# A hybrid decoder step on one core: some turned blocks as transposes, two key copies and two low-rank products side by side, a gate chunk split

## The reference, cut to what matters

```python
h  = rms_norm(x) * (1 + scale1) + shift1
q, k, v, p_rw, g_a, g_b = split(h @ w_in)
A  = sliding-window attention(q, k, v)           # window 128, T5 bias, sinks
xm = p_rw + (prev - p_rw) * mu                   # token shift
r, k, v, wl, al, gl = split(xm)
w_log = -softplus(-(w0 + tanh(wl) @ w_w2)) - 0.5 # decay: first low-rank product, 64 deep
decay = exp(-exp(w_log))
a     = sigmoid(a0 + al @ w_a2)                  # rate: second low-rank product, 64 deep
g     = sigmoid(gl) @ w_g2
k_mod = k * (1 + (a - 1) * k_a)
B  = scan over tokens of S = S*decay - (S kk)(kk a)^T + v k_mod^T, out S r; then group norm, * g
m  = sigmoid(g_a) * (A @ w_pa) + sigmoid(g_b) * (B @ w_pb)
x  = x + gate1 * (m @ w_o)
x  = x + gate2 * MoE(rms_norm(x) * (1 + scale2) + shift2)    # top 4 of 32 experts
```

## Time and profile before

| what | value |
|---|---|
| device time, median of 3 runs | 1280.71 us (1281.91, 1280.71, 1279.18) |
| span of the profiled execution, first to last instruction | 1276.6 us |
| granted TensorE clock, mean | 0.995 |
| PE busy | 1206.0 us (94%) |
| DVE busy | 455.5 us (36%) |
| ACT busy | 282.1 us (22%) |
| DMA, mean | 366 GB/s; 428 in the expert stage |
| chain that ended last | PE 66%, DMA 27%, ACT 3%, DVE 2% |

### The profile page before, as it was taken

One profiled execution on the slowest core, in us unless ns is written; L12 is line 12 of the kernel. 1 busy time (PEld: TensorE's weight loads), 2 busy tenths in 40 slices (PEclk: granted clock), 3 DMA queues, 4 the chain that ended last, 5 costly groups with the idle time before them and its releaser, 6 DMA issues.

```text
span 1276.6 us, 20795 instructions
## 1 busy us (share of the span) xinstructions
PE 1206.0 (94%) x8260; PEld 595.1 (47%) x8260; DVE 455.5 (36%) x1033; ACT 282.1 (22%) x525; POOL 53.2 (4%) x67
## 2 busy tenths in 40 slices
PE   7999999999999999999999999999998999999998
PEld 5887678788733333333333333333333333333333
DVE  3155756564442223322223333222222223332232
ACT  2013641120222112222122221121111122221211
POOL 0010624000000000000000000000000000000000
PEclk9999999999999999999999999999999999999999
DMA  9976331378699999999999999999999999999995
GB/s 362 367 275 245 116 105 70 102 256 317 248 394 422 421 429 427 428 426 429 429 428 428 428 429 429 430 428 428 428 428 430 429 429 428 428 428 428 428 428 236
DMA packets 56960, 467.24 MB, mean 366 GB/s; under 512 B 5197, under 2 KB 7505, under 8 KB 31802
## 3 DMA queue, kind: packets, MB, share of 16 engines
q1 hardware_dynamic: 54698, 461.10, 87.1%
q0 software_dynamic: 1664, 5.20, 1.5%
q10 hardware_dynamic: 544, 0.13, 0.0%
HBM read 463.94 MB, written 5.09 MB: 367 GB/s over the span
## 4 chain that ended last, share of the span: by engine, by line
PE 66%; DMA 27%; ACT 3%; DVE 2%; issue 1%; SPq 0%; POOL 0%; DVEq 0%; ACTq 0%
PE ps L1548 21%; DMA arena<-in_w 13%; DMA ring<-in_w 13%; PE ps L1569 12%; PE ps L965 5%; PE ps L1503 4%; PE ps L1477 3%; PE ps L955 2%; PE ps L1424 2%; PE ps L1392 2%; PE ps L1557 2%; PE ps L973 1%; PE ps L1484 1%; ACT PH L834 1%; PE ps L934 1%
## 5 line engine op out<-in xcount | busy, mean ns | idle before, releaser
L1548 PE MATMUL ps<-ring,PH 128*64 128x512 f32 x1536 | 340.9, 594 | 22.3 <-DMA ring<-in_w 22.1
L2140 DVE TENSOR_TENSOR SQ<-ps,SQ 128x528 f32<-128x528 f32 x124 | 79.1, 700 | 592.6 <-PE ps L1503 592.6
L1548 PEld LDWEIGHTS ps<-ring,PH 128*64 128x64 f32 x1536 | 108.3, 137 | 248.2 <-issue 200.4
L1569 PE MATMUL ps<-ring,PH 128*64 128x512 f32 x768 | 170.1, 595 | 0.3 <-DVE PH L2153 0.3
L829 ACT COPY PH<-ps 128x512 f32<-128x512 f32 x62 | 33.3, 589 | 393.2 <-PE ps L1548 393.2
L1548 PE MATMUL ps<-arena,PH 128*64 128x512 f32 x504 | 112.2, 594 | 8.2 <-DMA arena<-in_w 8.2
L1569 PEld LDWEIGHTS ps<-ring,PH 128*64 128x64 f32 x768 | 53.5, 137 | 99.9 <-issue 99.9
L1548 PEld LDWEIGHTS ps<-arena,PH 128*64 128x64 f32 x504 | 35.3, 137 | 83.3 <-issue 66.2
L1503 PE MATMUL ps<-PH 64*128 64x264 f32 x496 | 71.7, 408 | 0.0
L965 PE MATMUL ps<-PH,ring 128*128 128x264 f32 x304 | 69.3, 388 | 0.2 <-issue 0.2
L965 PEld LDWEIGHTS ps<-PH,ring 128*128 128x128 f32 x304 | 57.3, 190 | 10.7 <-issue 1.1
(11 more groups left out here) (475 smaller groups left out, 1101.7 us busy)
## 6 DMA issues: line engine op xcount, KB each, us to landing
ring<-in_w SPq DMA_DIRECT2D x144, 2048.0 KB, 31.5
arena<-in_w SPq DMA_DIRECT2D x46, 2048.0 KB, 31.5
ring<-in_w_mod SPq DMA_DIRECT2D x12, 2048.0 KB, 15.4
ring<-in_w_in SPq DMA_DIRECT2D x8, 2048.0 KB, 11.6
ring<-in_w_o SPq DMA_DIRECT2D x2, 2048.0 KB, 11.0
ring<-in_w_in SPq DMA_DIRECT2D x2, 1024.0 KB, 18.0
ring<-in_w_pa SPq DMA_DIRECT2D x1, 2048.0 KB, 8.6
ring<-in_w_pb SPq DMA_DIRECT2D x1, 2048.0 KB, 9.3
```

The lines of the kernel that those rows point to most:

```text
L1548: last = mm(ps[64 * lin:64 * lin + 64, 2 + hh, :], XG[:, k % 4, k // 4, :], slot_row(slot, c, k % 2, lin * FE + hh * 512), start=(k == 0), ...
L1569: last = mm(ps[64 * hh:64 * hh + 64, 4, :], AC[:, f, :], slot_row(slot, c, f % 4, hh * 512), start=(f == 0), stop=(f == NF - 1))
L2140: v.tensor_tensor(YA[:, p::4, :], ps[:, bank:bank + 2, 0:T], YA[:, p::4, :], ALU.add).then_inc(sem["comb_used"], 1)
```

## The change

It has four parts. The instructions of PE and ACT change as follows.

1. **Key copies adjacent.** Both `II` products are issued one behind the other after `sh_evac` has reached 4, and the two transposes follow.
2. **Low-rank products in pairs.** Decay and rate alternate, one on each row half of the array. ACT's sigmoids alternate too, and both of DVE's waits are now for all eight (`decay_rate`).
3. **Gate chunk split.** Three of its eight steps are issued after the first two pairs, five after the last two.
4. **Turned blocks as transposes.** In the three places the products whose output lies on partitions 0 to 63 get `is_transpose`: 8 of the 16 at L1162, 16 of the 32 at L1234 (8 in each batch), 4 of the 8 at L1355. Their partners on partitions 64 to 127 stay products.

```diff
-                   ("decay", 4), ("rate", 4), ("gate", 4), ("modT8", 1),
+                   ("decay_rate", 8), ("gate", 4), ("modT8", 1),
@@ ACT
                 act.activation(LD[:, hp, :], group(), ACT.Sigmoid, bias=par("rw_w0", hp)).then_inc(sem["a_evac"], 1)
-            for hp in range(4):
                 act.activation(Aa[:, hp, :], group(), ACT.Sigmoid, bias=par("rw_a0", hp)).then_inc(sem["a_evac"], 1)
@@ PE
+            pe.wait_ge(sem["sh_evac"], 4)
+            for kv in range(HKV):
+                mm(ps[:, 6 + kv, 0:T], II[64 * kv:64 * kv + 64, :], PTv[64 * kv:64 * kv + 64, CK, :], start=True, stop=True)
             for kv, (t0, nt) in enumerate(TILES[1:]):
-                pe.wait_ge(sem["sh_evac"], 3 + kv)
-                mm(ps[:, 6 + kv, 0:T], II[64 * kv:64 * kv + 64, :], PTv[64 * kv:64 * kv + 64, CK, :], start=True, stop=True)
                 tr(ps[0:nt, 6 + kv, T:T + P], PTv[:, CK, t0:t0 + nt], ID).then_inc(sem["kvrow_done"], 1)
@@
             for hp in range(4):
-                mm(group()[:, 0:T], LWw[0:64, hp * P:hp * P + P], XMv[0:64, 12, :], start=True, stop=True).then_inc(sem["a_done"], 1)
-            for hp in range(4):
-                mm(group()[:, 0:T], LWw[64:128, hp * P:hp * P + P], XMv[64:128, 12, :], start=True, stop=True).then_inc(sem["a_done"], 1)
-            gates(8)
+                for s in range(2):
+                    mm(group()[:, 0:T], LWw[64 * s:64 * s + 64, hp * P:hp * P + P], XMv[64 * s:64 * s + 64, 12, :],
+                       start=True, stop=True).then_inc(sem["a_done"], 1)
+                if hp % 2:
+                    gates(3 if hp == 1 else 5)
@@ L1162
-                                      start=True, stop=True)
+                                      start=True, stop=True, is_transpose=(q == 0))
@@ L1234
-                              start=True, stop=True)
+                              start=True, stop=True, is_transpose=(par == 0))
@@ L1355
-                          II[64 * s:64 * s + 64, 0:CH], start=True, stop=True)
+                          II[64 * s:64 * s + 64, 0:CH], start=True, stop=True, is_transpose=(s == 0))
@@ DVE
-            dve.wait_ge(sem["a_evac"], a_end("decay"))
+            dve.wait_ge(sem["a_evac"], a_end("decay_rate"))
...
-            dve.wait_ge(sem["a_evac"], a_end("rate"))
+            dve.wait_ge(sem["a_evac"], a_end("decay_rate"))
```

## The result

| | before | after |
|---|---|---|
| median of 6 runs each, us | 1280.83 (1277.72 to 1282.26) | 1289.28 (1284.62 to 1294.46) |
| span of the profiled execution, us | 1276.6 | 1285.6 |
| mean granted clock of PE in it | 0.995 | 0.993 |

The ratio is 1.0083, with a 95% interval of 1.0065 to 1.0101: the changed kernel is slower by 0.65 to 1.0%. That is 10.6 us (8.3 to 12.9); the two medians are 8.5 us apart, at the low end of this. The forecast was 1283.2 us and its range ended at 1286.4.

A forecast was written before the change was run, and what follows sets the result against it. Transfers (weight loads) bound the expert stage, so mixer-chain delay counts whole: +2.5 DVE's wait, +0.3 clock, -0.3 blocks, 0 copies and split, span 1276.6 to 1279.1; with 4.1 to the median, 1283.2 us, range 1279.2 to 1286.4.

The forecast's parts named there:

- DVE's wait: Mixer, low-rank products: DVE waits for the eighth sigmoid, L1772 starts at 130.29 instead of 127.81, +2.5 us (bounds +1.3, +3.3).
- Overlap of the row halves: Low-rank products on PE: two products on different row halves run side by side, 0.44 us a pair, second member 0.15 later.
- Key copies at nothing: Key copies on PE: adjacent copies save some 0.6 us, worth nothing because PE then waits for ACT's L651 anyway.
- The split at nothing of its own: Gate chunk split on PE: total unchanged, its earlier wait for the ring slot costs nothing since that load lands before 126.
- the sum: All terms: +2.5 DVE's wait, +0.3 clock, -0.3 blocks, 0 copies and split, together +2.5 us, giving 1283.2 us.
- Clock, +0.3 of 0 to 0.7: Gate steps from 136.14 on: PE idles longer, a 1.2 GHz stretch may follow; softmax chain loses 0 to 0.7 us, taken +0.3.
- Turned blocks, -0.3 of -0.5 to 0: L1162, L1234, L1355: transposes save records on PE, together -0.5 to 0 us, taken as -0.3.
- The second rival: Turned blocks: transposes in half-wide tiles cannot run beside their neighbours; 1285.8 us, or about 1295; chance 0.12.
- its dear form: Second rival: each transpose also pays 0.14 to 0.20 us on both sides, some 9 more, about 1295 us; within the 0.12.
- the cheap form: Second rival: transposes merely stand alone, +2.3 us in place of -0.3, 1285.8 us; within the 0.12.
- stalls that go: PE's 2.01 us stall at L1347 and both low-clock stretches vanish, 5.0 us won, 1278.2 us; chance 0.10.

The follow-up runs named there:

- the rest: The change with its three `is_transpose` taken out, against the kernel before: 1281.64 us, ratio 1.0016; with the gates unsplit as well: 1278.23 us, 1.0001.
- the inverse alone: The kernel before with transposes in the inverse batches (L1234) only, interleaved with products: 1286.75 us, ratio 1.0062.
- those with four groups: The kernel before with transposes in the inverse batches only, two at a time, four groups per batch: 1280.06 us, ratio 1.0017.

## Why the prediction was wrong

- **DVE's wait**: right. +2.5 us and L1772 at 130.29 were forecast; the change without transposes has 130.23, with the wait released by the sigmoids and ACT starving 1.06 us, as worked out. Its kernel is 2.0 us slower (0.5 to 3.6). That DVE's delay reaches the end whole, as the prediction took it, is not shown: without the split 1.20 us of the wait are left, and nothing in the time can be told from before.
- **Overlap of the row halves**: right, four products in 1.16 us.
- **Key copies at nothing**: right.
- **The split at nothing of its own**: wrong in the order of before, where it alone costs 3.1 us. The step looked only at the slot it waits for and at DVE. ACT's rates, which stand ahead of its later work, were treated as if only DVE waited for them. Inside the change the rest costs 2.0 us with the split and 0.1 without, and there the longer wait of DVE (2.36 against 1.20 us), which the sum did have, is part of the difference.
- **Clock, +0.3 of 0 to 0.7**: the place was right, the size not. The second softmax lost 1.67 us more than the first (3.73 against 2.06). The sixteen passes took 2.1 us longer and the score products ahead of them 0.5. The step had 1.2 to 1.8 us for a low stretch, from chunks of four and eight passes, and a slack of 0.91 us at L1087, which was gone. The 3.07 us behind the inverse were in no term at all. That the kernel without transposes came to +2.0 us, near the +2.8 of the sum without its blocks, is in part luck: its second softmax is 3.8 us late.
- **Turned blocks, -0.3 of -0.5 to 0**: the step that failed. They cost 10.7 us (8.1 to 13.3), of which the inverse alone 7.9. The bounds were made of records saved, and the rule against it, column tiling and the transpose mode exclude each other (the Trainium skill, "TensorEngine Tiling (Array Packing)", Restrictions and Gotchas), was set aside for the row of L1037. That row shows eight transposes one behind the other with a single turn ahead of them. It could not show a price paid at each turn, and the changed code goes to a transpose and back eight times in an inverse batch of 40 records. The transposes do run in half-wide tiles, so the rule as stated is too strong for this case, but it pointed at the place where the price was.
- **The second rival** came nearest, in its dear form: transposes that stand alone and pay 0.14 to 0.20 us on both sides. Measured are 0.17 and 0.20 us at L1163, and net for a group 0.37 us there, 0.26 at the inverse and 0.28 at L1356. It gave about 1295 and 1289 came. It was not right as a whole. Its price was for each transpose, and grouped transposes do not pay it, and it had nothing of the clock behind the batches. The price itself was in the sum's own rows: 0.14 to 0.20 us between tiles 64 and 128 rows deep. It had 0.12 together with the cheap form, and the range left it out.
- **Its opposite, stalls that go**: it came in part. Both low stretches went, worth about 1.6 us each, but the stalls only moved, from 3.70 to 2.76 us in all; the prediction counted one stall, where before has two large ones and after three. These 4.1 us were far less than was lost. No run shows that they belong to the change: twelve of the sixteen profiles have no low clock between 252 and 260 us.

What stays open: what a turn's price is made of; why the clock falls behind the interleaved batches, and not behind those with four groups; whether the small gain at L1162 is the clock's; and how much of the 0.1 to 0.2% differences depends on where the low stretches fall. Of the ten profiles in which the low-rank products stand one half after the other, eight have a low stretch between 124 and 136 us. The profile of before, on which the prediction was built, is one of the two without.

## What to carry to other kernels

A transpose in a half-wide tile of float32 is cheap in a row of its kind and dear between products: count the turns, 0.26 to 0.37 us each time there and back in these rows, not the records saved. When a single row is the evidence against a rule, ask whether it contains the situation as often as the new code will. And a filler chunk that is put between two halves of a producer can delay everything behind the second half on the consumer's engine, not only the wait that one has looked at.

## What was not expected of the hardware

PE can lose its clock while the windows count it as busy without a break (4.00 of 4.00 us, at 0.62 to 0.80, in the inverse alone); pauses show only in the weight loads, and that they are the cause is not shown. Grouping the same instructions keeps it at 1.00. The price per group was the same between one and four groups as between four and eight (0.263 and 0.265 us). And eight products that alternate between row halves take less time (a batch of 1.04 us) than transposes and products in groups (1.63 us), although these are eight passes fewer: in this batch running side by side is worth more than the shorter instruction.
